# Two norms of a fused block computed in two halves of the tokens, with the projection tiles around them

## The reference

```python
x = x + gate1 * (merged @ w_o[l])                       # tiles "wo"
h2 = rms_norm(x, norm2_w[l]) * (1.0 + scale2) + shift2  # norm "n2"
ff = jnp.square(jax.nn.relu(h2 @ w_mlp1[l])) @ w_mlp2[l]    # tiles "m1", "m2"
x = x + gate2 * ff
...
x = x + mla_layer(...)                                  # its last product: tiles "ob"
out = rms_norm_2(x, final_norm)                         # norm "fin"
```

## Time and profile before

| | us |
|---|---|
| median of 3 runs | 1614.76 (1613.32 to 1615.16) |
| the profiled execution | 1612.61 |
| its span, first to last instruction | 1610.8 |
| TensorE busy in it | 1575.7 (98%) |
| VectorE, ScalarE, GpSimd busy | 982.7, 761.9, 794.2 |

### The profile page before, as it was taken

How to read it: one execution, slowest core, us unless ns; L and a number is a source line. 1 busy time by engine, 2 the same in 40 slices (tenths; PEclk the granted TensorE clock), 3 DMA queues, 4 the chain that set the end, 5 groups by cost and what they waited for, 6 DMA issues and landing times. The chain is left out here.

```text
span 1610.8 us, 23675 instructions
## 1 busy us (share of the span) xinstructions
PE 1575.7 (98%) x8199; PEld 1291.5 (80%) x8199; DVE 982.7 (61%) x1316; ACT 761.9 (47%) x1389; POOL 794.2 (49%) x578
## 2 busy tenths in 40 slices
PE   7999999999999999999999999999999999999997
PEld 4778888888788788887878888888888878777776
DVE  4798888888549797587261321212278865557662
ACT  4675676676533644323343332324467646433332
POOL 0556666666646420256744444444644556334423
PEclk9999999999999999999999999999999999999998
DMA  8434434433322200467523333333332333211202
GB/s 317 123 123 125 131 113 117 138 113 118 106 87 77 60 27 1 144 236 249 162 75 102 92 105 92 101 96 92 98 93 79 103 100 106 69 55 53 66 23 89
DMA packets 76389, 171.29 MB, mean 106 GB/s; under 512 B 8256, under 2 KB 8640, under 8 KB 72832
## 3 DMA queue, kind: packets, MB, share of 16 engines
q1 hardware_dynamic: 68976, 133.09, 27.6%
q10 hardware_dynamic: 7312, 36.83, 6.4%
HBM read 167.67 MB, written 2.23 MB: 105 GB/s over the span
## 5 line engine op out<-in xcount | busy, mean ns | idle before, releaser
L606 POOL TENSOR_TENSOR w_lo<-w_raw,w_hi 128x512 fp32r<-128x512 f32 x455 | 661.9, 1476 | 554.7 <-ACT w_hi L654 554.1
L1175 PE MATMUL bank<-a_hi,w_hi 128*128 128x512 f32 x984 | 390.4, 397 | 2.3 <-ACT gates_early L719 1.2
L1177 PE MATMUL bank<-a_hi,w_lo 128*128 128x512 f32 x984 | 383.6, 390 | 0.0
L1176 PE MATMUL bank<-a_lo,w_hi 128*128 128x512 f32 x984 | 383.0, 389 | 0.0
L654 ACT ACTIVATE w_hi<-w_raw 128x512 fp32r<-128x512 f32 x457 | 263.8, 621 | 160.3 <-PE bank L1196 126.7
L1175 PEld LDWEIGHTS bank<-a_hi,w_hi 128*128 128x128 f32 x984 | 184.8, 188 | 43.8 <-issue 3.7
L1176 PEld LDWEIGHTS bank<-a_lo,w_hi 128*128 128x128 f32 x984 | 184.9, 188 | 39.3 <-issue 1.9
L1177 PEld LDWEIGHTS bank<-a_hi,w_lo 128*128 128x128 f32 x984 | 184.7, 188 | 39.5
L1193 PE MATMUL bank<-b_hi,w_hi 128*128 128x512 f32 x536 | 210.6, 393 | 3.0 <-DVE y_full L2344 1.8
L1196 PE MATMUL bank<-b_lo,w_hi 128*128 128x512 f32 x536 | 208.8, 390 | 0.0
L1194 PE MATMUL bank<-b_hi,w_lo 128*128 128x512 f32 x536 | 208.6, 389 | 0.0
(11 more groups left out here) (378 smaller groups left out, 2628.7 us busy)
## 6 DMA issues: line engine op xcount, KB each, us to landing
w_raw<-ws SPq DMA_DIRECT2D x457, 256.0 KB, 2.7
cs_rows<-cs_scratch ACTq DMA_DIRECT2D x16, 1024.0 KB, 5.1
ada_piece<-ada ACTq DMA_DIRECT2D x16, 1024.0 KB, 5.9
ada_piece<-ada SPq DMA_DIRECT2D x8, 1024.0 KB, 17.7
x_stream<-x SPq DMA_DIRECT2D x2, 1024.0 KB, 8.8
x_stream<-x ACTq DMA_DIRECT2D x1, 2048.0 KB, 8.0
out<-x_stream SPq DMA_DIRECT2D x8, 256.0 KB, 2.2
rope_table<-rope ACTq DMA_DIRECT2D x1, 512.0 KB, 4.3
```

The lines of the kernel that those rows point to most:

```text
L606: nc.gpsimd.tensor_tensor(wlo[b][:, :], raw[n % RAW_RING][:, :], r32(whi[b][:, :]), ALU.subtract)\
L1175: mm(out, lh, rh, start=first, stop=False)
L1176: mm(out, lh, rl, start=False, stop=False)
L1177: return mm(out, ll, rh, start=False, stop=last)
```

## The change

At the second norm, `wo` 6 and 7 are computed in two halves of 256 tokens, in the order 6 first half, 7 first, 6 second, 7 second. The sums, the root, the inverse and the rows are made for each half by itself, in banks 2 and 7, woven into these half tiles; `norm_split` becomes 16 steps of 256 tokens, and the pair of `m1` tiles takes them half by half. The fillers are gone, and ScalarE's preload of the root's table stands ahead of the rounding of the weights that `wo` 6 called for. At the final norm `ob` 6 and 7 are likewise computed in four halves; the scaling and the output go half by half, in 12 DMAs instead of 8. Half tiles are counted by semaphores that served once, early in the kernel. GpSimd's program is not edited, and neither are the values computed.

```diff
@@ names
+        HALF_SUMS, HALF_ROWS = (bank[2], bank[7]), (bank[2], bank[4])
...
+        def token_half(half):
+            return slice(half * SEQ // 2, (half + 1) * SEQ // 2)
@@ SyncE
-            for m in range(KT):
-                sp.wait_ge(fin_ready, m + 1)
-                sp.dma_start(d["out"][m], xF[:, m, :]).then_inc(s_out, 16)
-            sp.wait_ge(s_out, 16 * KT)
+            out = d["out"].rearrange("k p n -> p k n")
+            for half, step in ((0, 2), (1, 1)):
+                w = token_half(half)
+                for m in range(0, KT, step):
+                    sp.wait_ge(fin_ready, half * KT + m + step)
+                    sp.dma_start(out[:, m:m + step, w], xF[:, m:m + step, w]).then_inc(s_out, 16)
+            sp.wait_ge(s_out, 16 * (KT + KT // 2))
@@ ScalarE
-            for m in range(KT):
+            for m in range(KT - 2):
                 hi_upto(slab_of(("wo", m)) + AHEAD)
-                if m == KT - 1:
-                    A(small[:, 81:82], eps, ACT.Sqrt)
                 wait_evac(act, ("wo", m))
                 square("n2", m, xF[:, m, :])
                 if m == KT // 2 - 1:
                     keep_sums(2)
-            root("n2", 1.0 / D_MODEL)
-            for k in range(KT):
-                act.wait_ge(nfull, KT + k + 1)
-                A(aH[:, k, :], t[k % 2][:, :], ACT.Identity, bias=modc[:, 3 * KT + k:3 * KT + k + 1]).then_inc(hiA, 1)
+            A(small[:, 81:82], eps, ACT.Sqrt)
+            hi_upto(slab_of(("wo", KT - 2)) + AHEAD)
+
...
+            n0 = STAT_AT["n2"][0]
+            for m in (KT - 2, KT - 1):
+                act.wait_ge(sq_added, SQ_USED[n0 + m - 2][1])
+                act.wait_ge(half_added, OPENED + m - (KT - 2) + 1)
+                square_half(m, 0, half_sq)
+            act.wait_ge(half_summed, OPENED + 1)
+            root_of_half(0, half_root)
+            wait_evac(act, ("wo", KT - 2))
+            square_half(KT - 2, 1, sq_ready)
+            for j in range(2 * KT):
+                if j == 3:
+                    wait_evac(act, ("wo", KT - 1))
+                    square_half(KT - 1, 1, sq_ready)
+                if j == 6:
+                    act.wait_ge(stat_mm, SUM_AT["n2"])
+                    root_of_half(1, std_ready)
+                round_half(j)
+                if j in (0, 3):
+                    hi_upto(slab_of(("wo", KT - 1)) + AHEAD - (j == 0))
...
-            for m in range(KT):
+            A(small[:, 81:82], eps, ACT.Sqrt)
+            for m in range(KT - 2):
                 hi_upto(slab_of(("ob", m)) + AHEAD)
                 wait_evac(act, ("ob", m))
                 square("fin", m, xF[:, m, :])
-            root("fin", 1.0 / D_MODEL)
+            hi_upto(N_SLABS - 1)
+            for half in range(2):
+                w = token_half(half)
+                for m in (KT - 2, KT - 1):
+                    b, used = BANK_OF[("ob", m)]
+                    act.wait_ge(evac[b], used + 1 + half)
+                    n = STAT_AT["fin"][0] + m
+                    if half == 0:
+                        act.wait_ge(sq_added, SQ_USED[n - 2][1])
+                    A(sq[n % 2][:, w], xF[:, m, w], ACT.Square).then_inc(sq_ready, 1)
+                act.wait_ge(stat_mm, SUM_AT["fin"] + 2 * half)
+                A(roots_of_half(half), HALF_SUMS[half][:, 0:NCH // 2], ACT.Sqrt, bias=eps, scale=1.0 / D_MODEL)\
+                    .then_inc(std_ready, 1)
@@ TensorE
+                w, blocks = token_half(half), TILES[name][2]
+                for k, (b, o) in enumerate(weights(name)):
+                    ins = split_mm(gb(name)[:, w], whi[b][:, o:o + P], wlo[b][:, o:o + P], hi(k)[:, w], lo(k)[:, w],
+                                   k == 0, k == blocks - 1)
+                    if mid and k == blocks // 2 - 1:
+                        mid()
+                return ins
...
+            def n2_half_sums(half):
+                half_sums(sq_sum, half, True, False)
+                if half == 0:
+                    pe.wait_ge(half_sq, OPENED + 1)
+                    half_sums(sq[(n2_sq + KT - 2) % 2], 0, False, False)
+                else:
+                    pe.wait_ge(sq_ready, n2_sq + KT - 1)
+                    half_sums(sq[(n2_sq + KT - 2) % 2], 1, False, False).then_inc(stat_mm, 1)
...
+            start(before)
+            pe.wait_ge(rdyC, KT)
+            half_tile(before, 0, in_c, in_c_lo).then_inc(half_done, 1)
+            start(last)
+            pe.wait_ge(sq_added, POOL_AT["n2"] + KT - 3)
             pe.wait_ge(mod_ready, 2)
-            keep_clock(ADA, 9)
-            stat("n2", KT - 1)
-            keep_clock(ADA, 4)
-            rows("n2")
-            keep_clock(ADA, 9)
-
+            half_tile(last, 0, in_c, in_c_lo, lambda: n2_half_sums(0)).then_inc(half_done, 1)
+            half_tile(before, 1, in_c, in_c_lo, lambda: n2_last_sums(0)).then_inc(gemm_done, 1)
+            n2_half_rows(0)
+            half_tile(last, 1, in_c, in_c_lo, lambda: n2_half_sums(1)).then_inc(gemm_done, 1)
...
+                for half in range(2):
+                    w = token_half(half)
+                    for k, parts in enumerate(zip(*(weights(name) for name in names))):
+                        pe.wait_ge(hiA, N2_AT + half * KT + k + 1)
+                        for name, (b, o) in zip(names, parts):
+                            mm(gb(name)[:, w], whi[b][:, o:o + P], aH[:, k, w], start=(k == 0), stop=False)
+                            mm(gb(name)[:, w], wlo[b][:, o:o + P], aH[:, k, w], start=False, stop=False)
+                        pe.wait_ge(rdyA, N2_AT + half * KT + k + 1)
+                        for name, (b, o) in zip(names, parts):
+                            ins = mm(gb(name)[:, w], whi[b][:, o:o + P], aL[:, k, w], start=False, stop=(k == KT - 1))
+                            if half and k == KT - 1:
+                                ins.then_inc(gemm_done, 1)
+                        if half == 0 and k == 2:
+                            n2_last_sums(1)
+                        if half == 0 and k == 5:
+                            n2_half_rows(1)
...
+            for m in (KT - 2, KT - 1):
+                start(("ob", m))
+            half_tile(("ob", KT - 2), 0, in_a, in_a_lo).then_inc(gemm_done, 1)
+            half_tile(("ob", KT - 1), 0, in_a, in_a_lo, lambda: half_stat(0, KT - 2)).then_inc(gemm_done, 1)
+            half_tile(("ob", KT - 2), 1, in_a, in_a_lo, lambda: half_stat(0, KT - 1)).then_inc(gemm_done, 1)
+            half_rows(0)
+            half_tile(("ob", KT - 1), 1, in_a, in_a_lo, lambda: half_stat(1, KT - 2)).then_inc(gemm_done, 1)
+            half_stat(1, KT - 1)
+            half_rows(1)
@@ VectorE
+            for m in (KT - 2, KT - 1):
+                ve.wait_ge(half_done, OPENED + m - (KT - 2) + 1)
+                add_output(m, token_half(0)).then_inc(half_added, 1)
+            ve.wait_ge(half_root, OPENED + 1)
+            V.reciprocal(roots_of_half(0, "n2"), roots_of_half(0, "n2")).then_inc(half_inv, 1)
...
+            add_last_half(KT - 2)
+            ve.wait_ge(half_rows_in, OPENED + 1)
+            for j in range(2 * KT):
+                half, k = j // KT, j % KT
+                w = token_half(half)
+                if j >= 2:
+                    low_half(j - 2)
+                    ve.wait_ge(rdyA, N2_AT + j - 1)
+                if j == 3:
+                    add_last_half(KT - 1)
+                if j == 6:
+                    ve.wait_ge(std_ready, ROOT_AT["n2"] + 1)
+                    V.reciprocal(roots_of_half(1, "n2"), roots_of_half(1, "n2")).then_inc(rstd_ready, 1)
+                if j == KT:
+                    wait_rows("n2")
+                V.scalar_tensor_tensor(t[j % 2][:, 0:SEQ // 2], xF[:, k, w], gain2[:, k:k + 1], HALF_SUMS[half][:, w], ALU.mult, ALU.mult)\
+                    .then_inc(nfull, 1)
+            for j in (2 * KT - 2, 2 * KT - 1):
+                low_half(j)
...
+            add_half(KT - 2, 0)
+            add_half(KT - 1, 0)
+            inverse_of_half(0)
+            add_half(KT - 2, 1)
+            ve.wait_ge(rows_ready, ROOT_AT["fin"] + 1)
+            for m in range(KT - 1):
+                scale_half(m, 0)
+            add_half(KT - 1, 1)
+            scale_half(KT - 1, 0)
+            inverse_of_half(1)
             for m in range(KT):
-                add_to_stream(("ob", m), m)
-            inverse("fin")
-            wait_rows("fin")
-            for m in range(KT):
-                V.scalar_tensor_tensor(xF[:, m, :], xF[:, m, :], col("fin", m), PST[:, :], ALU.mult, ALU.mult)\
-                    .then_inc(fin_ready, 1)
+                scale_half(m, 1)
```

More of the change, by code:

```diff
@@ L1583, in _, with in_c, in_c_lo, half_tile @@
             turn_sums(1)
-            for m in range(KT):
-                feature_tile(("wo", m), lambda k: cH[:, k, :], lambda k: cL[:, k, :], (rdyC, 0),
-                             mid=(lambda: stat("n2", KT - 2)) if m == KT - 1 else None)
+            def in_c(k):
+                return cH[:, k, :]
```

(62 more changed lines are left out.)

96 lines of the change are left out of this document (57 added, 39 removed).

## The result

| | before | after |
|---|---|---|
| median of the runs timed together | 1613.3 (20 runs) | 1618.39 (20 runs) |
| ratio after / before, 95% interval | | 1.0028 [1.0020, 1.0035] |
| the profiled execution | 1612.61 | 1618.31 |
| its span | 1610.8 | 1616.5 |

The changed kernel is slower by 0.28%, about 4.5 us. The forecast was 0.9 us slower, which is too little to be told from no change. The measured time lies inside the range, by 0.1 us, on the side that had a chance of 0.07. The single times follow the mean granted clock: seven of the 20 runs after took 1614.4 to 1615.9 us at 0.995 to 0.997, the other thirteen 1617.8 to 1620.6, mostly at 0.992 to 0.993.

What follows compares the result with a forecast made beforehand. TensorE, busy for 98% of the span, was taken as the bound. Second norm +2.2 us and final norm -1.3 gave +0.9: 1615.7 us from a median of 1614.76, range 1611.0 to 1618.5.

Steps and rivals of the forecast that it cites:

- the side that had a chance of 0.07: Whole kernel: slower by over 0.2% (3.2 us), through the clock falling again; chance 0.07.
- The upper bound, 1618.5: Top of the forecast range for the whole kernel, set where the slower rival decides.
- The wait: Ahead of `wo` 7's first half: TensorE stands still 3.4 us for GpSimd's fifth addition of squares.
- The clock: Behind the stall ahead of `wo` 7: TensorE falls to 1.2 GHz, 2.7 us of it on work, 1.4 us lost.
- The bound of 1.7: Second norm: largest loss from the clock's fall, if all 3.4 us at half clock fall on work.
- The sums: Second and final norm: ten sums on TensorE at 0.106 us each, 1.06 us.
- +0.8: Second norm up to the tile after the pair: 0.8 us slower, without a fall of the clock.
- VectorE in the pair: `m1` pair: VectorE sets the pace, 16 steps of 0.91 us, 14.6 us for 11.6.
- The final norm: From `ob` 6 to the end: 1.3 us faster, between 0.3 and 1.8.
- The clock holds: Rival: no fall of the clock behind the stall at the second norm; -0.5 us, 1614.3; chance 0.27.
- the wait is covered: Rival: GpSimd's addition comes in time, `wo` 7 starts 3.4 us earlier; -3.9 us, 1610.9; chance 0.18.
- The slower rival: In the `m1` pair the clock falls again; two more stretches bring +3.5 us, 1618.3; chance 0.07.

Runs made afterwards that it cites:

- `second_only`: Changed kernel with only the second norm, `wo` 6 and 7 and the `m1` pair in halves, final norm as before the change; 1618.0 us, ratio to before 1.0027.
- `after_attn_fillers`: Changed kernel plus 17 filler matmuls in the waits at the start of the latent attention, nothing else; 1617.44 us, ratio to before 1.0019.
- `fillers`: Changed kernel with 18 filler matmuls on TensorE ahead of the wait of `wo` 7, the wait itself kept; 1615.0 us, ratio to before 1.0007.
- `no_stall`: Changed kernel with the root's table load behind the roundings and TensorE's wait for the added squares moved to the sums; 1612.28 us, ratio to before 1.0002.
- `no_stall_two_queues`: `no_stall` with four of the last eight output DMAs issued from ScalarE's queue; 1611.5 us, ratio to before 0.9991.
- `attn_fillers`: `no_stall_two_queues` plus 17 filler matmuls in the three waits at the start of the latent attention; 1610.7 us, ratio to before 0.9981.
- `table_behind`: Changed kernel with the square root's table loaded behind the rounding of the two slabs instead of ahead; 1615.13 us, ratio to before 1.0005.

## Why the prediction was partly wrong

**The number.** That the time fell inside the range is in part luck. The upper bound, 1618.5, was 3.7 us above the median that the forecast started from, 1614.76; beside the kernel before timed together with it (1613.3) the change cost 4.5.

**The wait.** Right in place, cause and size: 3.33 us against 3.4, through the same chain of table load, rounding, subtraction and addition. With the load behind the roundings it is 1.83, as the "1.9" of the prediction for an addition that is not delayed. ScalarE's next activation starts 1.29 us after the load begins, so a switch costs what the earlier trace rows showed. The 2.66 us of the Trainium skill (ScalarE: Activation LUTs, What ACT_TABLE_LOAD costs) would, as an estimate, have made the stall 4.8; the trace disagrees for a load placed like this one.

**The clock: the step that failed.** The prediction let the fall come "as late after the last wide matmul as there", as one stretch of 3.4 us, with 2.7 of it on work and 1.4 lost. The fall came, but lasted 6.8 us in the changed kernel's profile, 10.2 in `second_only` and 3.4 in `after_attn_fillers`, and the 6.8 us lay wholly on `wo` 7's work. Their price, from `fillers`, is 3.1 us. The bound of 1.7 was wrong too: it limited the length to that of the one fall in the earlier trace rows. Nor was the wait of the earlier trace rows the only long one in that trace, as the prediction says: TensorE also stood still for 2.61 us until 15.00, behind 24 fillers, and the 16 matmuls that followed ran at 2.4 GHz.

```profile
15.00 1.07 PE L1301 MATMUL bank<-ada_piece,small 128*32 128x256 f32 x16 [2.61 <-DMA ada_piece<-ada]
```

The price of a longer fall is read from the other profiles. With the stall in place, the time from `wo` 6 to the tile after the pair is 31.5, 32.8, 34.6 and 35.6 us for 0, 3.4, 6.8 and 10.2 us at 1.2 GHz; each stretch more costs 1.0 to 1.8. The Trainium skill (TensorE: Matmul & The Clock Gate, HAM oscillation) takes half of the time at the low clock as lost; by that, an estimate, 6.8 us would cost 3.4, and the 3.1 measured agree roughly.

**The sums: mis-sized.** The prediction has "ten sums at (804.24 - 802.54) / 16 = 0.106". But the x8 in the earlier trace rows is four chunks, not eight: a chunk's sum is two matmul records. Ten sums are 20 records; at that price they cost 2.1 us, 1.06 more, at each norm. In the profile after, a group of four records stands for two chunks. Without a fall the second norm came out at +1.7 (`fillers`), where the prediction had +0.8. The 0.9 between them: the stretch from `wo` 7's start to its end took 11.0 us instead of 10.5 (the sums 0.9 more, the transposes and half matmuls a little less), the one from there to the tile after the pair 14.2 instead of 13.7, and the stall 0.1 less than foretold.

**VectorE in the pair.** Right in the main: the steps start 0.91 us apart (timeline of VectorE after, beside the earlier trace rows), and from the end of `wo` 7 to the tile after the pair it takes 828.86 - 814.68 = 14.2 us, where the prediction's terms add up to 13.7. The 0.5 is spread over the start of the last addition, the wait for the second root and the last subtractions.

```profile
820.48 0.48 DVE L2414 SCALAR_TENSOR_TENSOR tmp<-x_stream,small,bank 128x256 f32<-128x256 f32 x1
820.87 0.48 DVE L2396 SCALAR_TENSOR_TENSOR a_lo<-tmp,small,a_hi 128x256 fp32r<-128x256 f32 x1
821.39 0.48 DVE L2414 SCALAR_TENSOR_TENSOR tmp<-x_stream,small,bank 128x256 f32<-128x256 f32 x1
```

**The final norm.** Foretold -1.3, measured -0.7. The last wide matmul ends 14.1 us after `ob` 6 starts instead of 13.4, mostly the sums again. From there to the first scaling 2.6 and the scalings' 3.2 are as predicted. SyncE's issues were wrongly taken at 0.33. The first of the last eight took that, the seven that queue behind it 0.43 to 0.45, one every 0.49, so the last is 0.6 late. As these smaller transfers land in 1.8 us instead of 2.2, the end moved by 0.2 alone.

**The rivals.** "The clock holds" and "the wait is covered" did not happen in the changed kernel; `fillers` and `no_stall` made them happen, and gave 3.1 and 6.1 us less than the changed kernel between `wo` 6 and the pair's end. The slower rival had the right mechanism, further stretches at 1.2 GHz, in the wrong place: it looked for them in the pair, where waits of 0.2 us brought none, instead of asking how long the first one would last where TensorE is the bound. Its chance of 0.07 was too low for that reason. The sum by terms from the profiles is +1.7 + 3.1 - 0.7 = 4.1 us, 0.25% of the time, beside the measured 4.5. The two need not agree so well, since the length of the fall differs between profiles; the fall at 1420 is in the profiled execution another 1.6.

## What to carry to other kernels

Where TensorE is the bound, price a new wait at its length plus the fall of the clock that may follow, and do not limit that fall to the length of one seen elsewhere: here a 3.3 us stall cost 3.1 more. Before splitting work into halves, follow what else is queued on the engines that release the first half; here a table load of 1.3 us, harmless in its old place, and a wait placed twelve half matmuls ahead of its use took more than the split could win. Fillers cost nothing in the wait that stood anyway (`wo` 7 started 6.3 us behind `wo` 6 with and without them), and several short waits in a row can bring the clock down too. And before dividing a stretch by its records, find out how many records one call makes: here a sum is two.

## What the hardware showed unasked

- The same stall of 3.33 to 3.43 us was followed by 3.4, 6.8 and 10.2 us at 1.2 GHz in three profiles, though TensorE worked without a pause from its end on. The fall came 2.2 us into the stall in `second_only`, 0.5 us ahead of its end in `after_attn_fillers`, and 1.5 us after its end in the changed kernel. Why it differs stays open.
- The length of a wait does not decide it. The wait of 2.6 us near 55 stands in all twelve profiles; the clock falls within or behind it in nine, and not in the changed kernel's, `second_only`'s and `no_stall_two_queues`'. The first two rows and the window are of the changed kernel: it also waited 3.45 us until 15.31, longer than the stall, and its next 16 matmuls took 1.07 us. In `attn_fillers` the same 16, at 1.2 GHz, took 1.94 behind a shorter wait (last row).

```profile
15.31 1.07 PE L1359 MATMUL bank<-ada_piece,small 128*32 128x256 f32 x16 [3.45 <-DMA ada_piece<-ada]
55.41 0.71 PE L1445 MATMUL bank<-a,consts 128*128 128x128 f32 x4 [2.58 <-DVE a L2118]
...
54.00:58.00 4.00, 2.59 (x24) 2.18 (x25) 3.83 (x8) 1.58 (x3) 0.00 (x0) 1.00 0.02 5
```

```profile
14.56 1.94 PE L1363 MATMUL bank<-ada_piece,small 128*32 128x256 f32 x16 [2.80 <-DMA ada_piece<-ada]
```

- Waits of 1.60, 0.63 and 1.69 us with short work between them were followed by a fall; one of 1.83 us alone (`table_behind`) was not, in its one profile.
- Falls also come at other places (near 14, 55, 437 and 1415 to 1420 in these profiles), in the profile of one kernel and not in that of another with the same code there. `attn_fillers`, the fastest by its ratio, has one of 10.2 us at 13.8 and one of 3.4 at 58.2, and its profiled execution is the slowest of its twelve. The times of single runs follow the mean clock, so these falls are likely much of the spread; how often each comes was not counted.
- An output DMA of 128 KB takes SyncE 0.43 to 0.45 us to issue where it queues directly behind another, and 0.34 where it does not (first row, the first of the last eight in the changed kernel). In `no_stall_two_queues`, where SyncE issues every other one, about 0.8 us apart, the same four took 0.33 or 0.34 (second row: all eight of its issues). So the longer time goes with the queueing, not with the rows of half the length.

```profile
1610.97 0.34 SPq L529 DMA_DIRECT2D out<-x_stream  x1
```

```profile
L529 SPq DMA_DIRECT2D out<-x_stream x8: 332/358/404, 1599.1 to 1607.2; - x8
```
